# A hand-written order of work on one core: the delta rule's steps of the first head begin after class unit 9 instead of unit 13

## The chip, the core and the metric

One NeuronCore of a Trainium2 chip runs the whole program. The metric is the device time of one execution in microseconds (us); lower is better. All data is float32. Engines are named as in the profile: PE (TensorE, matrix multiplications), PEld (its weight loads), DVE (VectorE), ACT (ScalarE), POOL (GpSimd) and SP (SyncE, which here only issues transfers).

## The reference

One layer of a decoder with two mixers that work in parallel on the same normalised input, for a prompt of 2048 tokens and for 8 sequences of 4 new tokens. Cut to what the change touches, the prompt's mixers are:

```python
def hybrid_layer(x, ...):
    h = rmsnorm(x, norm_g)
    proj = jnp.einsum('bld,de->ble', h, w_in)
    # mixer a: gated delta rule, 4 heads of 128, evaluated in chunks
    qkv = causal_short_conv(x_ext, conv_w)
    o_a, s_new = gated_delta_rule(qa, ka, va, g, beta, s0)
    o_a = rmsnorm(o_a, dn_norm_g) * silu(z_a)
    # mixer b: causal windows at dilations 1, 4 and 16, 8 heads of 64, softmax merged over all three
    parts = [dilated_branch_prompt(qb, kb, vb, w // d, d) for w, d in DILATIONS]
    o_b = merge_dilations(parts) * silu(z_b)
    y = x + jnp.einsum('ble,ed->bld', concat(o_a, o_b), w_out)

def gated_delta_rule(q, k, v, g, beta, s0):      # per chunk
    sol = triangular_solve(eye + a_mat, rhs)     # needs the inverse of a unit lower triangle
    u, w = sol[..., :dv], sol[..., dv:]
    def step(S, xs):                             # strictly one chunk after the other
        v_new = u_c - w_c @ S
        o_c = q_c @ S + a_c @ v_new
        S = S * gl + k_c.T @ v_new
```

## The kernel before

The program has five stages, separated by barriers: `project` (the input projection), `gates`, `mixers`, `sample` and `output`. The change lies in `mixers`.

`mixers` handles the prompt in 16 chunks of 128 tokens (mixer a) and 8 attention heads (mixer b). It pairs them: while attention head h is finished, two delta chunks, 2h and 2h+1, are computed. Before the first head a preparation runs over all 16 chunks (`prepare`): decay matrices, key products, and the scores of head 0.

Each engine walks through the same list of steps in its own program (`walk`, L1189), and does in each step what is its part. An engine executes its instructions in the order in which they are written; a wait for a semaphore holds back everything that is written behind it. The list for the first head is `OPENING = head_order(True, True)` (L1063), for the others `BODY`. So `head_order` (L885) alone sets the order around the change. It makes two lists and weaves them:

- the attention steps. `turn k` transposes the k-th of 18 units of the exponentiated scores on PE (L1427), ACT evacuates it to `pt` and then issues one of 14 copies of the sample caches, DRAM to DRAM (`shift`, L1493 to L1496). `mix k` multiplies it with the values on PE (L1449), two units later. `score q` computes the q-th unit of the scores of the next head on PE (L1390 to L1397), and DVE scales and masks them (L1625, L1631); PE may be two score units ahead of DVE. `close r` adds two partial results on DVE (L1681), and POOL multiplies them with the gate (L1270). `near b` evacuates on ACT (L1529). `spread`, `swap` and `peak` form the row maxima of the next head.
- the 33 delta steps of `DELTA_ORDER` (L935), for chunk u of 0 and 1: three levels of `cross` (PE L1320, DVE L1579) and `double` (PE L1329 and L1330, DVE L1585 and L1587), which build the inverse of the 128-row triangle from inverses of its 16-row diagonal blocks; then the chain of the state, `ks`, `solve`, `av`, `su`, `qs` (PE L1339, L1353, L1364, L1358, L1347), and the norm of the output, `norm` (POOL L1252 to L1261) and `turn_o` (PE L1369, DVE L1613). `grow` is POOL's: it lays the 16-row inverses of the next chunk into a zeroed square (L1229).

The 16-row inverses of all chunks come from a substitution that only the opening has: the steps `sub` 1 to 15 and `flip` on DVE (L1567, L1569, L1674), which are ahead of `turn 8`. Their result is reordered through DRAM: SP writes it out (L1108, L1110), waits until both writes have landed, and reads it back in another shape (L1114). Meanwhile POOL, after the writes, zeroes `cross` (L1274), then waits for the reads and grows chunks 0 and 1 (L1229). Only then can PE start the first `cross` (its waits are at L1311 to L1314).

The delta steps are woven in by cost: each attention step has a cost in `head_order` (4 for a `turn`, 5 for a `score`, 8 for a `mix`, 10 each for the last three), and after each attention step as many delta steps are given as the share of the cost spent so far demands. In the opening the costs of all steps ahead of k = `FIRST_DELTA` are set to nothing, so that the delta steps begin there and are spread evenly over what is left:

```python
        if opening and k == FIRST_DELTA:
            cost = [0] * len(cost)
```

Of the kernel before, what the change touches and what calls it, by code (L numbers as in the profile page):

```python
# [843 lines left out]
LATEST = (1, 1, 3, 3, 5, 5, 7, 7) + (12,) * 5 + (17,) * 5  # L844
# [33 lines left out]


SUBS = 8  # L880
FIRST_NEAR = 9
FIRST_DELTA = 13


def head_order(more, opening=False):  # L885

    order, cost = [("exp", 0)], [0 if opening else 18]

    def add(c, *step):
        order.append(step)
        cost.append(c)

    for k in range(UNITS + LAG):
        if opening and k == FIRST_DELTA:
            cost = [0] * len(cost)
        if opening and 0 < k <= SUBS:
            for row in range(2 * k - 1, min(2 * k + 1, BASE)):
                add(0, "sub", row)  # L900
        if opening and k == SUBS:
            add(0, "flip")
        if k < UNITS:
            add(4, "turn", k)
            if k in FIRST and k != FIRST[-1]:
                add(0, "exp", FIRST.index(k) + 1)
            if more:
                for q in range(UNITS):
                    if k == (LATEST[q] if q >= 8 else FIRST_NEAR + q // 2 if opening else LATEST[q] + q % 2):
                        add(5, "score", q)  # L910
        if k >= LAG:
            m = k - LAG
            add(8, "mix", m)
            if m < 8 and m % 2:
                add(0, "near", m // 2)
            if m in (12, 17):
                for r in (0, 1) if m == 12 else (2, 3):
                    add(0, "close", r)
    if more:
        add(10, "spread")  # L920
        add(10, "swap")
        add(10, "peak")

    delta = [("delta",) + s for s in DELTA_ORDER if more or s[0] != "grow"]
    woven, spent, given = [], 0, 0
    for step, c in zip(order, cost):
        woven.append(step)
        spent += c
        upto = len(delta) * spent // sum(cost)
        woven += delta[given:upto]  # L930
        given = upto
    return woven
# [82 lines left out]
def mixers(nc, env, D):  # L1015

    with ExitStack() as ctx:
# [42 lines left out]
        shifted = sem("shifted")  # L1060
        S_CREDIT, T_CREDIT, C_CREDIT = 2, UNITS, 4
        BODY = [head_order(True), head_order(False)]
        OPENING = head_order(True, True)  # L1063
        PAIRS = SW_HEADS // 2
        block = ctx.enter_context(nc.Block())
# [1482 lines left out]
```

How the kernel before makes its waits and increments, by code:

```python
def at_least(eng, sem, n):  # L79
    if n > 0:
        eng.wait_ge(sem, n)
# [83 lines left out]
        @block.sync  # L166
# [11 lines left out]
            def load_x(n):  # L178
                if n >= XS:
                    sp.wait_ge(xT_done, 2 * (n - XS) + 2)
                if n < NT:
                    sp.dma_start(x_slot[n % XS], D.x[P * n:P * n + P, :]).then_inc(x_loaded[n % XS], 16)
                else:
                    sp.dma_start(x_slot[n % XS][0:NS, :], D.x_sample).then_inc(x_loaded[n % XS], 16)
# [1 line left out]
            def store_rows(n):  # L186
                sp.wait_ge(t_out, n + 1)
                sp.dma_start(D.new_v[P * n:P * n + P, :], stage[:, n % 2, :]).then_inc(stage_stored[n % 2], 16)
# [16 lines left out]
            with nc.allow_non_contiguous_dma(reason="a few weights, once"):  # L205
                for r in range(CONV_W):
                    sp.dma_start(conv_wt[:, :, r], D.conv_w[r].rearrange("(t p) -> p t", p=P)).then_inc(consts_in, 16)
            load_x(7)
            for n in range(8, NT + 1):
                load_x(n)
                store_rows(n - 8)
            load_w(1)
            for n in range(NT - 7, NT):
                store_rows(n)
            sp.wait_ge(v_sam_out, 1)
            for b in range(DEC_BATCH):
                sp.dma_start(D.out_v[b, PAST - DEC_SEQ:PAST, :], stage[DEC_SEQ * b:DEC_SEQ * b + DEC_SEQ, 0, :]).then_inc(rows_out, 16)
            def store_turned(j, kind, c):
                sp.wait_ge(tok_done, posts_before(j, kind, c) + 1)
                dst = {"k": D.k_tok, "v": D.v_tok, "wk": D.new_k}[kind]
```

## Time and profile before

| what | us |
|---|---|
| median of three runs | 2018.37 |
| lowest and highest run | 2014.06, 2027.25 |
| the profiled execution | 2027.25 |
| its span, first to last instruction in the profile | 2025.5 |

The profiled execution is the slowest of the three runs, 8.9 us above the median. It shows 27,818 instructions. PE is the engine with the most busy time. A busy PE in this profile is not a PE at its peak, since the clock that it is granted has two levels, shown in the views as 1.00 (2.4 GHz) and 0.50 (1.2 GHz), or as a mean between them for a stretch that has both. A timeline line gives the start, the length, the engine, the line of the kernel, what is written and read, how many like instructions were merged, and in brackets the idle time before it with what ended it. PE's instructions overlap, so the time from one start to the next says more than the length.

### The profile page before, as it was taken

To read this page: it belongs to the slowest core of one execution; us is meant where nothing else is said; L and a number is where in the kernel's file an instruction comes from. 1 tells how busy PE (TensorE), PEld (TensorE's weight loads), DVE (VectorE), ACT (ScalarE), POOL (GpSimd) and SP (SyncE) were. 2 spreads that over 40 slices of the span, in tenths; PEclk is the share of its full clock that TensorE was granted. 3 is DMA by queue.
4 is the path that set the end of the run, shared out by engine and by line. 5 is a ranking of instruction groups with operands and counts; after the bars stand their busy time and mean duration, and the time that the engine had idled before them with its cause. 6 is when DMAs were issued, how large, how long until landed. Compare 5 with 4: busy or idle time off the path is not lost. (4 is left out here: it accounts for less than half of the span.)

```text
span 2025.5 us, 27818 instructions
## 1 busy us (share of the span) xinstructions
PE 1745.5 (86%) x9674; PEld 1445.1 (71%) x9674; DVE 818.2 (40%) x1890; ACT 644.2 (32%) x1547; POOL 355.1 (18%) x367
## 2 busy tenths in 40 slices
PE   1999999999999999705788998998899468888897
PEld 1998888888888888604677887787788346666674
DVE  3424412511531351053743434544443445454462
ACT  3423311412321231111222443443444213333341
POOL 0000000000000000015123223313422343224231
PEclk9999999999999999958877988988998658999999
DMA  6321233344235333369774897797767456665660
GB/s 136 116 70 57 86 100 88 73 94 112 66 85 116 75 73 100 73 137 275 213 217 134 272 276 217 232 294 238 229 200 235 131 159 179 198 196 154 185 186 32
DMA packets 250191, 309.24 MB, mean 153 GB/s; under 512 B 70268, under 2 KB 198780, under 8 KB 240588
## 3 DMA queue, kind: packets, MB, share of 16 engines
q1 hardware_dynamic: 246484, 240.66, 44.5%
q10 hardware_dynamic: 3584, 66.98, 9.2%
q8 instruction: 72, 1.18, 0.2%
q14 instruction: 51, 0.42, 0.1%
HBM read 228.01 MB, written 146.44 MB: 185 GB/s over the span
## 5 line engine op out<-in xcount | busy, mean ns | idle before, releaser
L314 PE MATMUL pj<-hT_hi,w_hi 128*128 128x512 f32 x896 | 359.1, 401 | 1.8 <-DVE raw L541 1.8
L316 PE MATMUL pj<-hT_hi,w_lo 128*128 128x512 f32 x896 | 351.9, 393 | 0.0
L315 PE MATMUL pj<-hT_lo,w_hi 128*128 128x512 f32 x896 | 351.6, 392 | 0.0
L316 PEld LDWEIGHTS pj<-hT_hi,w_lo 128*128 128x128 f32 x896 | 168.3, 188 | 38.1
L314 PEld LDWEIGHTS pj<-hT_hi,w_hi 128*128 128x128 f32 x896 | 168.4, 188 | 36.8 <-issue 2.1
L315 PEld LDWEIGHTS pj<-hT_lo,w_hi 128*128 128x128 f32 x896 | 168.6, 188 | 34.5
L1449 PE MATMUL o_ps<-pt,vt 128*65 128x256 f32 (+3 forms) x560 | 154.4, 404 | 3.1 <-DVE ot L1681 2.1
L648 POOL IOTA row_at<- 128x1 int32 x1 | 0.1, 138 | 875.1 <-POOLq L2488 875.1
L1518 ACT ACTIVATE pt<-pt_ps 128x512 f32<-128x512 f32 x144 | 84.5, 587 | 184.3 <-PE pt_ps L1427 183.6
L2214 PE MATMUL y_bank<-wo_hi,mh 128*128 128x512 f32 (+1 forms) x272 | 113.4, 417 | 6.8 <-POOL ml L2199 4.6
L2215 PE MATMUL y_bank<-wo_lo,mh 128*128 128x512 f32 (+1 forms) x272 | 110.5, 406 | 0.0
L509 DVE SCALAR_TENSOR_TENSOR acc<-raw,conv_wt,acc 128x512 f32<-128x512 f32 x144 | 108.3, 752 | 5.1
L2216 PE MATMUL y_bank<-wo_hi,ml 128*128 128x512 f32 (+1 forms) x272 | 109.9, 404 | 0.0
L1449 PEld LDWEIGHTS o_ps<-pt,vt 128*65 128x65 f32 x560 | 75.4, 146 | 35.9 <-issue 25.0
L560 DVE TENSOR_TENSOR lo<-pj,hi 128x512 fp32r<-128x512 f32 x32 | 22.1, 692 | 156.5 <-ACT hi L472 156.5
L498 DVE TENSOR_TENSOR w_lo<-w_raw,w_hi 128x1024 fp32r<-128x1024 f32 x28 | 34.3, 1225 | 107.4 <-ACT w_hi L385 107.4
L1330 PE MATMUL d_ps<-tri,cross 128*128 128x64 f32 x384 | 76.9, 308 | 0.0
L1511 ACT ACTIVATE sc_near<-sc_near,ntop 128x256 f32<-128x256 f32 (+1 forms) x128 | 53.7, 490 | 68.3 <-DVE ntop L1660 65.6
L460 ACT ACTIVATE sil<-acc 128x512 f32<-128x512 f32 x48 | 30.4, 632 | 139.5 <-DVE acc L509 139.5
L1320 PE MATMUL d_ps<-tri,d_nt 128*128 128x64 f32 x384 | 61.7, 317 | 14.9 <-issue 8.9
L1631 DVE CUSTOM_DVE_ANT_0 sc_class<-s_ps,class_tab 128x512 f32<-128x512 f32 (+3 forms) x128 | 58.9, 488 | 32.4 <-PE s_ps L1397 21.9
L1320 PEld LDWEIGHTS d_ps<-tri,d_nt 128*128 128x128 f32 x384 | 59.8, 237 | 17.0 <-issue 16.9
(450 smaller groups left out, 3521.7 us busy)
## 6 DMA issues: line engine op xcount, KB each, us to landing
out_dram<-in_cache_k_win_dram ACTq DMA_DIRECT2D x56, 584.0 KB, 7.0
out_dram<-in_cache_v_win_dram ACTq DMA_DIRECT2D x56, 584.0 KB, 6.2
w_raw<-in_w_in_dram SPq DMA_DIRECT2D x32, 512.0 KB, 7.9
qk_ch<-sil SPq DMA_DIRECT2D x32, 256.0 KB, 2.4
z_ch<-xr SPq DMA_DIRECT2D x32, 256.0 KB, 2.5
wqk<-hi SPq DMA_DIRECT2D x32, 256.0 KB, 2.6
wqk<-lo SPq DMA_DIRECT2D x32, 256.0 KB, 2.9
sc_class<-qk_ch SPq DMA_DIRECT2D x32, 256.0 KB, 4.5
```

What stands on the lines that cost most here:

```text
L314: pe.matmul(out, w_hi[s][:, k, :], hT_hi[:, k, cols], start=(k == 0), stop=False)
L315: pe.matmul(out, w_hi[s][:, k, :], hT_lo[:, k, cols], start=False, stop=False)
L316: mm = pe.matmul(out, w_lo[s][:, k, :], hT_hi[:, k, cols], start=False, stop=(k == KT - 1))
L509: dve.scalar_tensor_tensor(out=a, in0=x(r), scalar=w(r), in1=a, op0=ALU.mult, op1=ALU.add).then_inc(chain if r < CONV_W - 1 else conv_done, 1)
L1320: mm = pe.matmul(d_ps[u][:, 64 * n:64 * n + 64], nt[u][:, n, :], blocks(tl[u], l, 0)[:, n], start=True, stop=True)
L1330: mm = pe.matmul(d_ps[u][:, 256 + 64 * n:256 + 64 * n + 64], x[:, n, :], blocks(tt[u], l, 1)[:, n], start=True, stop=True)
L1449: mm = pe.matmul(o_ps[g % 2][0:HD + 1, P * first:P * first + w], vt[:, n, :], pt[:, k % CUTS, at:at + w], start=opened, stop=False, skip_g ...
L1518: act.activation(pt[:, k % CUTS, 0:w], pt_ps[k % 2][:, 0:w], ACT.Copy).then_inc(S["turned_out"], 1)
L1631: ins = dve.tensor_tensor_reduce(sc_class[:, r, class_at(b):class_at(b + 1)], s_ps[k % 2][:, at:at + w], E.class_tab[:, CHUNK - w:], SCALE ...
L2214: pe.matmul(y_ps[0:rows, :], mh[:, u, k, 0:rows], w_hi[:, k, cs], start=(k == 0), stop=False)
L2215: pe.matmul(y_ps[0:rows, :], mh[:, u, k, 0:rows], w_lo[:, k, cs], start=False, stop=False)
L2216: mm = pe.matmul(y_ps[0:rows, :], ml[:, u, k, 0:rows], w_hi[:, k, cs], start=False, stop=(k == KT - 1))
```

## The change

`FIRST_DELTA` goes from 13 to 9, and the constant `FIRST_NEAR`, which was 9 and sets where the first score units of head 1 stand, is replaced by `FIRST_DELTA`, so that the score units keep their places. All that moves are the 33 delta steps of the opening. The list of `BODY` is the same. The file has one line less, so that all lines behind it have a number smaller by one in the changed kernel.

```diff
 SUBS = 8
-FIRST_NEAR = 9
-FIRST_DELTA = 13
+FIRST_DELTA = 9
...
-                    if k == (LATEST[q] if q >= 8 else FIRST_NEAR + q // 2 if opening else LATEST[q] + q % 2):
+                    if k == (LATEST[q] if q >= 8 else FIRST_DELTA + q // 2 if opening else LATEST[q] + q % 2):
```

The opening from `flip` on, as the function gives it before (exp, near and rest left out, of which the last does nothing on any engine; `x:u` is a delta step x of chunk u):

```text
flip turn8 mix6 turn9 score0 score1 mix7 turn10 score2 score3 mix8 turn11 score4 score5 mix9 turn12 score6..score12 mix10
turn13 cross0:0 mix11 cross0:1 double0:0 turn14 double0:1 mix12 cross1:0 cross1:1 turn15 double1:0 mix13 double1:1 cross2:0
turn16 cross2:1 mix14 double2:0 double2:1 turn17 ks:0 score13 qs:0 score14 solve:0 score15 score16 av:0 su:0 score17 mix15
ks:1 norm:0 mix16 solve:1 mix17 turn_o:0 qs:1 close close spread su:1 av:1 swap grow:1 norm:1 peak turn_o:1
```

and now:

```text
flip turn8 mix6 turn9 score0 cross0:0 score1 mix7 cross0:1 turn10 double0:0 score2 double0:1 score3 mix8 cross1:0 turn11
cross1:1 score4 double1:0 score5 mix9 double1:1 turn12 cross2:0 score6 cross2:1 score7 score8 double2:0 score9 double2:1
score10 score11 ks:0 score12 qs:0 mix10 solve:0 turn13 mix11 turn14 av:0 mix12 su:0 close close turn15 grow:0 mix13 ks:1
turn16 mix14 norm:0 turn17 solve:1 score13 score14 score15 turn_o:0 score16 qs:1 score17 mix15 su:1 mix16 av:1 mix17
grow:1 close close spread norm:1 swap turn_o:1
```

On PE, from `turn 9` on (first row; `pt_ps` is where it is turned to). The rows with `s_ps` are scores, those with `o_ps<-pt,vt` are `mix 7`. Before:

```order
L1427 MATMUL pt_ps<-ident,sc_class 128x128 x4
L1390 MATMUL s_ps<-kh,qs 128x128
L1391 MATMUL s_ps<-kl,qs 128x128
L1390 MATMUL s_ps<-kh,qs 128x256
L1391 MATMUL s_ps<-kl,qs 128x256
L1390 MATMUL s_ps<-kh,qs 128x256
L1391 MATMUL s_ps<-kl,qs 128x256
L1390 MATMUL s_ps<-kh,qs 128x256
L1391 MATMUL s_ps<-kl,qs 128x256
L1449 MATMUL o_ps<-pt,vt 65x256
L1449 MATMUL o_ps<-pt,vt 65x128 x2
L1427 MATMUL pt_ps<-ident,sc_class 128x128 x4
```

and in the changed kernel:

```order
L1426 MATMUL pt_ps<-ident,sc_class 128x128 x4
L1389 MATMUL s_ps<-kh,qs 128x128
L1390 MATMUL s_ps<-kl,qs 128x128
L1389 MATMUL s_ps<-kh,qs 128x256
L1390 MATMUL s_ps<-kl,qs 128x256
L1319 MATMUL d_ps<-tri,d_nt 128x64 x4
L1389 MATMUL s_ps<-kh,qs 128x256
L1390 MATMUL s_ps<-kl,qs 128x256
L1389 MATMUL s_ps<-kh,qs 128x256
L1390 MATMUL s_ps<-kl,qs 128x256
L1448 MATMUL o_ps<-pt,vt 65x256
L1448 MATMUL o_ps<-pt,vt 65x128 x2
```

The first `cross` (`d_ps<-tri,d_nt`) now stands behind four rows of scores; before it stood 60 rows further down, behind `turn 13`.

On PE, from `mix 15` to the end of the first head (`L1369` and then `L1368` are `turn_o`, `wide,fold` is `swap`). Before:

```order
L1449 MATMUL o_ps<-pt,vt 65x512
L1339 MATMUL d_ps<-d_state,kq 128x128 x4
L1449 MATMUL o_ps<-pt,vt 65x384
L1449 MATMUL o_ps<-pt,vt 65x128
L1353 MATMUL d_ps<-four,tri 128x128 x4
L1449 MATMUL o_ps<-pt,vt 65x256 x2
L1369 MATMUL d_ps<-ident,d_oo 128x128 x4
L1347 MATMUL d_ps<-d_state,kq 128x128 x4
L1358 MATMUL d_ps<-four,ktok 128x128 x4
L1364 MATMUL d_ps<-four,d_attn 128x128 x4
L1405 MATMUL s_ps<-wide,fold 128x64 x2
L1369 MATMUL d_ps<-ident,d_oo 128x128 x4
```

and in the changed kernel, to `turn_o` of chunk 1:

```order
L1448 MATMUL o_ps<-pt,vt 65x512
L1357 MATMUL d_ps<-four,ktok 128x128 x4
L1448 MATMUL o_ps<-pt,vt 65x384
L1448 MATMUL o_ps<-pt,vt 65x128
L1363 MATMUL d_ps<-four,d_attn 128x128 x4
L1448 MATMUL o_ps<-pt,vt 65x256 x2
L1404 MATMUL s_ps<-wide,fold 128x64 x2
L1368 MATMUL d_ps<-ident,d_oo 128x128 x4
```

The last `mix` is now followed by `swap` and `turn_o` alone; before, four more delta steps stood between.

On POOL, the end of the first head, from the product that `su` of chunk 1 needs (`four<-four,dl`). `zb` are the two gates of `close`, the rows with `ors` and `d_oo` are `norm` of chunk 1. Before:

```order
L1242 TENSOR_TENSOR four<-four,dl 128x512
L1270 TENSOR_TENSOR zb<-ot,zb 64x512 x2
L1229 TENSOR_TENSOR tri<-inv_t,own 128x512
L1229 TENSOR_TENSOR tri<-inv_l,own 128x512
L1252 TENSOR_TENSOR ors<-oss,rq 128x4
L1255 TENSOR_SCALAR ors<-ors 128x4
L1257 TENSOR_TENSOR ors<-ors,halves 128x4
L1259 TENSOR_TENSOR ors<-ors,rq 128x4
L1261 TENSOR_TENSOR d_oo<-d_oo,ors 128x512
```

and in the changed kernel:

```order
L1241 TENSOR_TENSOR four<-four,dl 128x512
L1228 TENSOR_TENSOR tri<-inv_t,own 128x512
L1228 TENSOR_TENSOR tri<-inv_l,own 128x512
L1269 TENSOR_TENSOR zb<-ot,zb 64x512 x2
L1251 TENSOR_TENSOR ors<-oss,rq 128x4
L1254 TENSOR_SCALAR ors<-ors 128x4
L1256 TENSOR_TENSOR ors<-ors,halves 128x4
L1258 TENSOR_TENSOR ors<-ors,rq 128x4
L1260 TENSOR_TENSOR d_oo<-d_oo,ors 128x512
```

`grow` now stands ahead of the gates; `norm` stands behind them in both.

## Rows read from the trace of the kernel before

**Rows 1.** Part 1 of the page, busy time of each engine.
```profile
PE 1745.5 (86%) x9674; PEld 1445.1 (71%) x9674; DVE 818.2 (40%) x1890; ACT 644.2 (32%) x1547; POOL 355.1 (18%) x367
```

**Rows 2.** Timeline of PE around the first inverses; start, length, engine, line, operation, idle before.
```profile
1017.11 0.31 PE L1390 MATMUL s_ps<-kh,qs 128*128 128x128 f32 x1
...
1017.65 0.28 PE L1390 MATMUL s_ps<-kh,qs 128*128 128x256 f32 x1
...
1020.50 0.30 PE L1390 MATMUL s_ps<-kh,qs 128*128 128x128 f32 x1 [0.90 <-DVE top L1625]
...
1033.42 0.60 PE L1427 MATMUL pt_ps<-ident,sc_class 128*128 128x128 f32 x4
1039.91 1.94 PE L1320 MATMUL d_ps<-tri,d_nt 128*128 128x64 f32 x8 [5.89 <-issue]
```

**Rows 3.** Timelines of DVE, SP and POOL, the same stretch.
```profile
1018.76 1.04 DVE L1674 COPY cross<-cross 128x1024 f32<-128x1024 f32 x1
...
1019.83 0.33 SPq L1110 DMA_DIRECT2D inv_all<-cross  x1
...
1029.37 2.70 POOL L1274 MEMSET cross<- 128x1536 f32 x2 [53.14 <-DMA inv_all<-cross]
1037.75 1.05 POOL L1229 TENSOR_TENSOR tri<-inv_t,own 128x512 f32<-128x512 f32 x1 [5.67 <-DMA inv_l<-inv_all]
```

**Rows 4.** Timeline of ACT, two of three cache copies that it issues there.
```profile
1019.64 0.54 ACTq L1496 DMA_DIRECT2D out_dram<-in_cache_v_win_dram  x1
...
1025.72 0.52 ACTq L1496 DMA_DIRECT2D out_dram<-in_cache_v_win_dram  x1
```

**Rows 5.** DMA view of 1018 to 1030 us; packets, MB, share of 16 engines.
```profile
q10 hardware_dynamic: 194, 3.44, 73.8%
q1 hardware_dynamic: 288, 1.05, 21.6%
```

**Rows 6.** Stretches; us, busy and count by engine, granted clock, DMA share, GB/s.
```profile
1018.00:1040.00 22.00, 14.08 (x80) 11.26 (x78) 11.12 (x50) 7.62 (x15) 4.95 (x5) 0.91 1.00 322
1040.00:1073.70 33.70, 33.70 (x144) 30.24 (x145) 6.75 (x16) 1.79 (x3) 7.81 (x7) 0.50 0.38 85
1073.70:1100.00 26.30, 19.07 (x130) 16.82 (x129) 14.86 (x43) 7.03 (x29) 15.96 (x19) 0.95 0.44 104
...
1102.00:1114.70 12.70, 12.23 (x55) 11.68 (x56) 3.23 (x13) 5.00 (x11) 0.64 (x1) 0.50 0.94 308
1173.90:1185.60 11.70, 10.06 (x46) 9.70 (x47) 2.59 (x11) 6.47 (x15) 2.04 (x2) 0.50 0.96 331
```

**Rows 7.** Timeline of PE, the same kinds of step at each clock.
```profile
1061.69 1.92 PE L1449 MATMUL o_ps<-pt,vt 128*65 128x512 f32 x2
1063.40 0.52 PE L1329 MATMUL d_ps<-cross,tri 128*128 128x64 f32 x2
...
1120.95 1.02 PE L1449 MATMUL o_ps<-pt,vt 128*65 128x256 f32 x4
1121.81 0.33 PE L1329 MATMUL d_ps<-cross,tri 128*128 128x64 f32 x2
```

**Rows 8.** Timeline of PE, the end of the first head.
```profile
1088.52 1.03 PE L1449 MATMUL o_ps<-pt,vt 128*65 128x256 f32 x4
...
1094.28 0.56 PE L1405 MATMUL s_ps<-wide,fold 128*128 128x64 f32 x4
1100.31 1.11 PE L1369 MATMUL d_ps<-ident,d_oo 128*128 128x128 f32 x4 [5.47 <-POOL d_oo L1261]
```

**Rows 9.** Timelines of DVE and POOL, the same end.
```profile
1090.69 1.27 DVE L1681 TENSOR_TENSOR ot<-o_ps,ot 65x512 f32<-65x512 f32 x2
...
1091.45 3.65 POOL L1270 TENSOR_TENSOR zb<-ot,zb 64x512 f32<-64x512 f32 x2 [0.77 <-DVE ot L1681]
...
1097.11 0.19 POOL L1252 TENSOR_TENSOR ors<-oss,rq 128x4 f32<-128x4 f32 x1
...
1099.21 1.04 POOL L1261 TENSOR_TENSOR d_oo<-d_oo,ors 128x512 f32<-128x512 f32 x1
```

## The prediction

> **What bounds the kernel now.** I read the busy times first, then the granted clock in stretches, then the timeline of PE around the place of the change, and only then the other engines there. PE has 86% of the span in busy time, the next engine 40% [rows 1]. In the opening head the timeline of PE is nearly gapless but for two holes: 5.89 us ahead of the first `cross` at 1039.91, and 5.47 us ahead of the last `turn_o` at 1100.31 [rows 2, 8]. Since every head follows on PE's one list, a delay of that last `turn_o` should delay all behind it. So I take its start as the mark: 1100.31 before, and the change is worth what it moves that mark.
>
> The first hole is the way of the 16-row inverses. DVE's `flip` ends at 1018.76 + 1.04 = 1019.80; SP issues the second write at 1019.83; the writes have landed when POOL is released at 1029.37; the reads when it starts `grow` at 1037.75 [rows 3]. PE's `cross` follows after two of POOL's four `grow` operations of 1.05 us each, at 1039.91 [rows 2]. That way takes 20.1 us from the end of `flip`, and nothing on PE's list shortens it. In the kernel before, PE fills 14 us of it, to 1034.0, with score units, turns and mixes [rows 2].
>
> The reader is to see a second thing in the stretches: after that hole PE has a clock of 0.50 (1.2 GHz) from 1040 to 1073.7, for 33.7 us, although it is busy for all of them [rows 6]. What it does there is `cross` and `double`, with a mix or a turn between. In the next heads, where scores, turns and mixes are interleaved with the same steps, the low level holds for 12.7 us (1102 to 1114.7) and 11.7 us (1173.9 to 1185.6) [rows 6].
>
> **The change, part by part.**
>
> *The work that loses its cover.* PE now reaches `cross` at 1017.65, behind the first score unit, and stands until the inverses have come [rows 2]. What it did from there to 1034 must be done later: score units 1 to 12, mixes 7 to 10, turns 10 to 13. Between 1018 and 1040 PE is busy for 14.08 us [rows 6]; nothing between 1034 and 1039.91 is in that. So +14.1 us, at the full clock. DVE, ACT and POOL have nothing that could go ahead: their scores, evacuations and gates all wait for PE.
>
> *The way of the inverses gets shorter.* In it ACT issues three cache copies (turns 10 to 12), from 1019.64 to 1025.72 [rows 4]. They now come behind PE's wait. From 1018 to 1030 the queue of these copies (q10) held the 16 DMA engines for 73.8% of 12 us with 3.44 MB, and SP's queue (q1), which has the inverses, for 21.6% [rows 5]. One copy of 584 KB is then 0.584/3.44 x 8.86 = 1.5 us of all engines, three are 4.5 us. The bounds are 0 (the transfers wait for memory, not for engines) and -4.5 us. I take -3, since the writes landed 9.5 us after their issue in this crowd. The first `cross` then starts at about 1036.9, and PE stands for 19 us where it stood for 5.9.
>
> By the Trainium skill (DMA: Bandwidth & Descriptors, section "Issuing engines are not separate DMA queues") transfers that different engines start interleave on the same 16 DMA engines. The shares of the two queues above agree, and by the rule alone the term would be the whole -4.5.
>
> *The clock.* After the longer hole PE will again be at 1.2 GHz. Then it meets `cross`, a score unit, a mix, `cross`, a turn, `double`, a score unit and so on, which resembles the later heads, where the low level held for 12 us [rows 6]. I take 15 us, some more than there, since the new list has fewer turns between the delta steps than those heads. At the low level a mix takes 63.40 - 61.69 = 1.71 us from start to start, at the high one 121.81 - 120.95 = 0.86 us (times above 1000) [rows 7], so a microsecond at the low level does half a microsecond's work. Before: 33.7 us low. Saved: (33.7 - 15)/2 = -9.4 us. Bounds: at 12 us low, -10.9; at 34 us low, 0.
>
> *Small waits in the middle.* From 1073.7 to 1100 PE is idle for 26.30 - 19.07 = 7.2 us, of which 5.5 are the second hole, so 1.8 us are small waits [rows 6, 8]. In the new order `close`, `grow` and `norm` of chunk 0 come right after each other on POOL, at 3.65 + 2.1 + 3.1 us [rows 9, 3], behind `mix 12`, and PE has about 8 us of work from there to `turn_o` of chunk 0. Laying the lists of PE, DVE and POOL beside each other with these durations, I get 2.4 us of waiting there, and some 0.8 us at score units 8 to 11, where PE waits for DVE's masks as it does at 1020.50 for 0.90 us [rows 2]. That makes 3.2 against 1.8: +1.4 us, with 0 and +4 as bounds.
>
> *The second hole.* `norm` of chunk 1 waits in both orders behind POOL's two gates, which wait for the last mix. The last mix starts at 1088.52 and ends about 0.9 us later, and `turn_o` comes at 1100.31, 10.9 us behind its end, of which 5.47 are idle [rows 8]. Now `turn_o:0`, `qs`, `su` and `av` stand ahead of that mix and no longer fill the time. From its end: about 0.3 us of signalling and DVE's first addition (half of 1.27 us), POOL's two gates (3.65 us), then `norm` 3.1 us (1097.11 to 1100.25) [rows 9], and about 0.2 to signal PE, in all 7.9 us, with half a microsecond of `swap` in it. The hole is about 7.5 us where it was 5.5: +2.0 us. `grow`, which stood between gates and `norm`, is ahead of them now; that gain of 2.1 us is in the 7.9.
>
> The sum is 14.1 - 3 - 9.4 + 1.4 + 2.0 = +5.1 us for the profiled execution, from 2027.25 to 2032.4. Its time is 8.9 us above the median of the runs shown, and nothing of that lies in the terms, so I put the same difference to the median: 2018.4 + 5.1 = 2023.5 us. Nothing in the later heads changes its order, and their transfers keep their distance from the mark.
>
> **The rivals.**
>
> *The clock stays low (slower than forecast).* The mark of 33.7 us came from a stretch with one mix and one turn in about ten microseconds (four mixes from 1041 to 1072, of which [rows 7] has one). If sparse scores aren't enough to change that, PE stays at 1.2 GHz through all of `cross` and `double`, 34 us or more. The clock term is then 0, and the sum +14.5 us: 2033. For it speaks that this stretch was fully busy and still low; against it that two heads with nearly the same mixture rose after 12 us.
>
> *The clock comes back at once, and the delta steps are covered (faster).* In this case the low level lasts for some 3 us. The saving is (33.7 - 3)/2 = 15.4 us, the round trip gives all of its 4.5, and the small waits stay as they are: 14.1 - 4.5 - 15.4 + 0 + 2.0 = -3.8 us, 2014.6. It decides from a low stretch of under 11 us on: there 14.1 - 4.5 - 11.6 + 2.0 is zero. Against it is that no head's beginning rose sooner than after 11.7 us.
>
> The Trainium skill (TensorE: Matmul & The Clock Gate, section "What's actually happening") has it that the gate opens after sustained work of PE. By that rule this rival would hold, with 2014.6; but the 33.7 busy microseconds at 0.50 [rows 6] don't agree with it, and the measurement decides.
>
> *The order is absorbed.* A later wait could eat the delay, for instance the operands of the next chunks. Then nothing is seen: 2018.4. Against it: in the next head PE is busy 12.23 of 12.70 us right after the mark [rows 6], so there is no slack to take it.
>
> *The change doesn't do what it says.* If `cross` did not wait for the inverses, the wait at 1017.65 would not arise and only the interleaving would be left, about -9 us. The code excludes it: the wait for POOL's `grow` is ahead of it.
>
> **How the numbers follow.** Main case 0.55, clock low 0.2, clock back at once 0.13, absorbed 0.1, something unnamed 0.02. A measurement of this kernel can tell about 1% from no change, 20 us; its own three runs lie within 13. The terms' own bounds give 14.1 - 4.5 - 10.9 + 0 + 1 = -0.3 at one end and, with 22 us low, 14.1 + 0 - 6 + 4 + 3 = +15 at the other; with the rivals and some microseconds of scatter of a median the range is 2011 to 2036 us. Slower by over 1% (above 2038.6) needs the low clock and bad luck: 0.07. Faster by over 1% (below 1998) has no term that would carry it: 0.02. Within 1%: 0.91.
>
> **What would show each step.** Right: PE's first `cross` comes directly behind one score unit, with an idle time of 18 to 22 us ahead of it and its start near 1037; no cache copy is issued in this hole; the low clock from about 1021 on lasts some 15 us beyond the first `cross`; `turn_o` of chunk 0 waits about 2 us for POOL, that of chunk 1 about 7.5; the mark lies near 1105 to 1107. The next heads look as before, shifted. Wrong: an inverse that lands before 1034 or after 1040 (the transfer term), a low level of under 8 or over 25 us after `cross` (the clock term), a mark that has moved by 5 us without the total following (the absorbed case).

## The result and the profile after

The changed kernel takes 2026.17 us (median of 12 runs, 2023.1 to 2029.8), the kernel before in runs beside it 2014.42 us (12 runs, 2006.9 to 2027.3). The ratio is 1.0053 with a 95% interval of 1.0035 to 1.0072: slower by about 11 us, within 1%. The forecast was 2023.5 us with a range of 2011 to 2036 and a difference of +5.1.

The two profiled executions, however, are equally long: a span of 2025.5 us before and of 2025.1 after. So a comparison of these two traces can't show where 11 us come from. What it does show is that PE's waits came where the prediction put them, and that the clock did not do what it said. PE in the opening head after the change, as a timeline (start, length, engine, line, operation, idle before it with its releaser):

```profile
1016.67 0.28 PE L1390 MATMUL s_ps<-kl,qs 128*128 128x256 f32 x1
1035.77 1.94 PE L1319 MATMUL d_ps<-tri,d_nt 128*128 128x64 f32 x8 [18.82 <-issue]
...
1083.94 1.12 PE L1368 MATMUL d_ps<-ident,d_oo 128*128 128x128 f32 x4 [1.97 <-POOL d_oo L1260]
...
1095.71 0.66 PE L1404 MATMUL s_ps<-wide,fold 128*128 128x64 f32 x4 [1.75 <-DVE wide L1641]
1101.70 1.12 PE L1368 MATMUL d_ps<-ident,d_oo 128*128 128x128 f32 x4 [5.33 <-POOL d_oo L1260]
```

These answer to [rows 2, 8]. The first `cross` stands behind one score unit and waits for 18.82 us where it waited for 5.89. `turn_o` of chunk 0 now waits for POOL's `norm`, 1.97 us. `turn_o` of chunk 1 waits for 5.33 us behind `swap`, which itself waited for 1.75.

The way of the inverses, from the timelines of DVE, SP and POOL, against [rows 3]:

```profile
1017.61 1.04 DVE L1673 COPY cross<-cross 128x1024 f32<-128x1024 f32 x1
...
1018.67 0.33 SPq L1109 DMA_DIRECT2D inv_all<-cross  x1
1026.18 0.37 SPq L1113 DMA_DIRECT2D inv_t<-inv_all  x1
...
1033.61 1.05 POOL L1228 TENSOR_TENSOR tri<-inv_t,own 128x512 f32<-128x512 f32 x1 [4.70 <-DMA inv_l<-inv_all]
```

The writes land 7.5 us after their issue, where it was 9.5, and from `flip` to the first `cross` it is 1035.77 - 1017.61 = 18.16 us, where it was 21.15.

The clock in stretches, against [rows 6] (us; busy time and count of PE, PEld, DVE, ACT, POOL; granted clock, DMA share, GB/s):

```profile
1035.77:1042.40 6.63, 6.63 (x29) 6.25 (x30) 1.59 (x6) 0.59 (x1) 4.91 (x5) 0.50 1.02 219
1042.40:1083.00 40.60, 37.88 (x275) 34.20 (x273) 21.68 (x77) 10.88 (x28) 8.88 (x11) 1.00 0.38 104
1083.00:1090.30 7.30, 6.36 (x23) 5.25 (x24) 2.31 (x9) 1.14 (x4) 3.91 (x4) 0.53 0.45 131
```

Behind the hole PE is at 1.2 GHz (0.50) for 6.6 us only, and then again for 6.9 us, nearly all of the third stretch, behind the new wait of `turn_o`; before it was 33.7 us in one piece. A low stretch of under 8 us after `cross` was one of the prediction's own signs that its clock term was wrong. The mark, the start of the last `turn_o`, lies at 1101.70 and not at 1105 to 1107.

In what follows, three starts are the marks in each trace: F, DVE's copy that ends the inverses (`flip`); C, PE's first `cross`; M, the `turn_o` of chunk 1 in the opening head. "Low behind C" is how long the granted clock stays at 0.50 behind C, read in stretches of 0.5 us.

### The profile page after: what moved, and what is told of

Its sections match the earlier page's. It is cut to its first block and busy times, and to the rows that moved or that the text cites. A ratio compares the mean times of both kernels' runs of the same rounds, so it can differ in the third digit from the quotient of the medians.

```text
span 2025.1 us, 27818 instructions
## 1 busy us (share of the span) xinstructions
PE 1734.0 (86%) x9674; PEld 1435.7 (71%) x9674; DVE 818.3 (40%) x1890; ACT 644.4 (32%) x1547; POOL 355.2 (18%) x367
## 5 line engine op out<-in xcount | busy, mean ns | idle before, releaser
L1510 ACT ACTIVATE sc_near<-sc_near,ntop 128x256 f32<-128x256 f32 (+1 forms) x128 | 53.7, 490 | 71.3 <-DVE ntop L1659 68.7
L1329 PE MATMUL d_ps<-tri,cross 128*128 128x64 f32 x384 | 71.6, 291 | 0.0
```

Source lines behind the costliest of these rows:

```text
L1329: mm = pe.matmul(d_ps[u][:, 256 + 64 * n:256 + 64 * n + 64], x[:, n, :], blocks(tt[u], l, 1)[:, n], start=True, stop=True)
```

## The experiments

Each kernel ran on a chip beside the kernel before; `b_` kernels start from the kernel before, `a_` kernels from the changed one.

**b_again and b_again2: the kernel before, unchanged.** No edit.

> The kernel before, unchanged, profiled once more. Theory (clock): the 12 times of before reach from 2006.9 to 2027.3 us, those of the changed kernel only from 2023.1 to 2029.8, because in before PE's low clock after the 5.9 us hole lasts for a different time from execution to execution. The profiled execution of 2027.25 us had 33.7 us of it. One that takes 2010 to 2016 us should show a low stretch shorter by twice the difference, 5 to 14 us, and the rest alike. Rival (elsewhere): the scatter of before comes from transfers or from other stages; then a faster execution shows about 34 us at the low clock again and is shorter in another place.

> The kernel before once more, for a third look at the clock. Clock theory: from the copy that ends the inverses (flip) to the last turn_o of the opening head the time is 65.5 us (what b_warm shows without any low clock there) plus half of the low stretch behind the hole (10 us gave 70.1, 37.5 us gave 81.6), so that this profile too lies on that line within 1.5 us. Rival: some other value with the same low stretch.

b_again: median 2017.45 us of 12 runs, 2005.4 to 2032.7, ratio 1.0021 (0.9987 to 1.0055), which is the kernel against itself. Its profiled execution took 2011.2 us. The view of stretches and the timeline of PE:

```profile
1041.85:1047.00 5.15, 5.15 (x21) 4.33 (x21) 0.42 (x1) 0.00 (x0) 3.92 (x4) 0.50 1.02 215
1047.00:1084.50 37.50, 34.06 (x253) 30.64 (x252) 20.24 (x57) 6.82 (x26) 16.60 (x17) 1.00 0.40 91
...
1088.60 1.12 PE L1369 MATMUL d_ps<-ident,d_oo 128*128 128x128 f32 x4 [5.48 <-POOL d_oo L1261]
```

The low clock behind C lasts 5.2 us here where the first profile of the same kernel had 33.8. From C to M it is 46.75 us instead of 60.40, and the time is 16 us lower. The second repeat, b_again2 (one execution, 2024.3 us), has

```profile
1040.89:1057.00 16.11, 16.11 (x70) 14.61 (x71) 2.35 (x6) 0.60 (x1) 3.92 (x4) 0.51 0.78 164
...
1092.71 1.11 PE L1369 MATMUL d_ps<-ident,d_oo 128*128 128x128 f32 x4 [5.47 <-POOL d_oo L1261]
```

16.1 us of low clock, and 51.82 us from C to M. F to M is 72.5 us. The line of the expectation counts the low clock within the hole too, some 17 us in all, and gives 74.0, so this profile is just within its 1.5. The first profile is not: 65.5 plus half of its 37.5 us would be 84.3, and it has 81.6. The three traces are of the same program, with the same wait ahead of M (5.47 and 5.48 us). So the kernel before has a lottery in its opening head, and the profile that the prediction was made from had drawn the worst of three. It isn't the only lottery: b_again2 has 17.7 us less of the low clock behind C than the first profile and 9.0 us less from F to M, but it is only 3.0 us faster. Its F comes 1.4 us later, and what follows M takes 4.6 us more (929.8 us for 925.2).

**b_warm and a_warm: the hole filled.** PE gets matmuls whose result nobody reads, just ahead of the first `cross`; nothing is left out.

```diff
+        OPENING.insert(OPENING.index(("delta", "cross0", 0)), ("warm", 24))      # a_warm: 80
...
+                elif step == "warm":
+                    for _ in range(a[0]):
+                        pe.matmul(d_ps[0][:], E.ident_r[:], heads(E.shut), start=True, stop=True)
```

> Before, with 24 matmuls of 128x512 whose results nobody reads put on PE ahead of the first cross of the opening head, into the 5.9 us hole (about 5.2 us of work). Clock theory: PE keeps 2.4 GHz behind the hole, the time is about that of the fastest executions of before, 2005 to 2009 us, and its scatter is under 8 us. Rival (elsewhere): median within 3 us of before's 2014 and the scatter still 15 to 20 us.

> The changed kernel, with 80 such matmuls in the 18.8 us hole ahead of its first cross (about 17.3 us of work). The clock is taken out on both sides, so that a_warm against b_warm is the price of the order alone. By the prediction's terms without the clock that is 14.1 (work that lost its cover) - 3.7 (inverses earlier, as seen) + 1.4 + 2.0 = about +14 us, so a_warm at 2019 to 2024 us. Against the changed kernel it saves half of the 6.6 us low stretch behind the hole, 3 us. Rival (the delta chain gains from sitting between attention steps): a_warm is only 3 to 8 us above b_warm, since at the full clock the packed order of before waits more for DVE.

In the traces both kept the clock at 2.4 GHz from the start of `cross` on. In b_warm it falls only in the wait ahead of M, where PE has nothing to do. In a_warm it falls once more, for 3.4 us of work behind the wait of the first `turn_o` (the last line shown of a_warm):

```profile
1036.91 1.08 PE L1321 MATMUL d_ps<-tri,d_nt 128*128 128x64 f32 x8 [0.18 <-issue]
...
1081.40 1.12 PE L1370 MATMUL d_ps<-ident,d_oo 128*128 128x128 f32 x4 [5.48 <-POOL d_oo L1262]
...
1036.91:1077.50 40.59, 36.86 (x272) 32.87 (x272) 20.85 (x59) 7.02 (x27) 20.72 (x21) 1.00 0.51 125
...
1293.00:1320.00 27.00, 25.52 (x112) 23.89 (x113) 6.79 (x25) 9.41 (x21) 2.65 (x3) 0.50 0.97 281
```

```profile
1035.89 1.08 PE L1320 MATMUL d_ps<-tri,d_nt 128*128 128x64 f32 x8 [0.88 <-issue]
...
1080.90 0.66 PE L1369 MATMUL d_ps<-ident,d_oo 128*128 128x128 f32 x4 [1.97 <-POOL d_oo L1261]
...
1097.81 1.12 PE L1369 MATMUL d_ps<-ident,d_oo 128*128 128x128 f32 x4 [5.33 <-POOL d_oo L1261]
...
1035.89:1083.00 47.11, 43.46 (x315) 39.52 (x316) 24.40 (x84) 11.48 (x29) 16.83 (x19) 1.00 0.49 120
1083.00:1086.50 3.50, 3.50 (x13) 2.42 (x12) 1.17 (x8) 1.14 (x4) 0.87 (x1) 0.53 0.84 237
```

F starts at 1015.98 in b_warm and at 1017.80 in a_warm. F to M is then 65.4 us against 80.0: the new order costs 14.6 us, where the prediction's terms without the clock gave 14.5. From C to M it is 44.49 against 61.92, that is +17.4, and from F to C 20.93 against 18.09, that is -2.8. Part of this is clock even so: 3.4 us of work at half the speed are 1.7 us. Without them the order costs 12.9 us, of which +15.7 lie from C to M. The rival that expected 3 to 8 us, because the packed order of before should wait more for DVE, falls.

The times did less. b_warm has a median of 2014.49 us (ratio 0.9996, 0.9964 to 1.0028) and still runs from 2006.9 to 2026.1: my expectation of 2005 to 2009 was wrong, and the rival, a median within 3 us of before and the same scatter, describes the times. The last line of b_warm's stretches gives a reason for the execution that was profiled: a later head, the fourth behind the opening, stayed at 1.2 GHz for 27 us, where heads usually have 10 to 14. What the other eleven executions had, no trace shows. a_warm has 2021.56 us (ratio 1.0022, 0.9996 to 1.0049), inside its range, and lies 7 us over b_warm; with this scatter the medians can't confirm the 14.6 us of the traces. That was left to the runs with the clock held everywhere.

**a_norm: POOL's order at the end.** The changed kernel with

```diff
+        OPENING.remove(("delta", "norm", 1))
+        OPENING.insert(OPENING.index(("close", 2)), ("delta", "norm", 1))
```

> The changed kernel with one delta step moved: in the opening, norm of chunk 1 stands ahead of the last two close steps, as in the list of the later heads, so that POOL does not do two gates (3.65 us) ahead of it. If POOL's order makes the second hole (5.3 us ahead of the last turn_o), the time falls by about 3 us, 2023 us, and the hole is 2 to 2.5 us, PE then waiting for ACT's squares and the norm alone. Rival: the hole is set by the squares of ACT anyway, and nothing moves.

```profile
1098.32 1.11 PE L1370 MATMUL d_ps<-ident,d_oo 128*128 128x128 f32 x4 [2.35 <-POOL d_oo L1262]
```

The wait ahead of M falls from 5.33 to 2.35 us, so POOL's two gates ahead of `norm` make 3 us of that hole. F to M falls from 84.1 to 81.5 us, which alone would prove little, since a_again below, without the edit, has 81.7; but the low clock is as long here as in the first profile of the changed kernel (6.9 us behind `cross`, and another 6.9 later). The time, 2025.12 us (ratio 1.0045, 1.0015 to 1.0076), for 2023 expected, has moved by 1 us against the changed kernel, which the interval doesn't tell from none or from three.

**b_copies: the cache copies out of the way.** In the kernel before, for head 0 alone:

```diff
+                    if isinstance(h, int) and h == 0 and 10 <= k <= 12:
+                        k = 2 * PIECES
+                    elif isinstance(h, int) and h == 0 and k >= 15:
+                        k -= 5
```

> Before, with the three cache copies of turns 10 to 12 issued with turns 15 to 17 instead, so that they are out of the way of the inverses. If they cost the way of the inverses what the changed kernel's trace shows (19.3 against 16 to 17 us from the copy of DVE to POOL's grow), the first cross comes 3 us earlier and the hole shrinks from 6 to 8 us to 3 to 5. The low clock behind it stays a matter of luck, or is shorter on average with a shorter hole. Median 3 to 6 us below before. Rival (the way waits for memory, not for engines): the time from flip to grow stays at 19 us, and nothing moves.

```profile
1018.67 0.33 SPq L1110 DMA_DIRECT2D inv_all<-cross  x1
1027.51 0.37 SPq L1114 DMA_DIRECT2D inv_t<-inv_all  x1
...
1037.08 1.94 PE L1320 MATMUL d_ps<-tri,d_nt 128*128 128x64 f32 x8 [3.73 <-issue]
```

The writes land 8.8 us after their issue, where the three traces of before have 9.5, 12.0 and 10.7 us. With F at 1017.58, F to C is 19.50 us, against 21.15, 23.39 and 20.72 before and 18.16 in the changed kernel. So by this one trace the copies are about 2 us of the 3 to 4 that the inverses gained, against a scatter of 2.7 us before; the rest is open. The hole was 3.73 us and the clock was low behind it all the same, for 15.9 us. Median 2013.57 us beside 2018.55, ratio 0.9973 (0.9939 to 1.0007): 5 us less, as expected (3 to 6), but the interval doesn't tell it from nothing.

**fd11 and fd15: other places.** `FIRST_DELTA` at 11 and at 15, `FIRST_NEAR` left at 9.

> Before with FIRST_DELTA = 11, the score units kept: the first cross stands behind score 4, about 5 us of PE's work later than in the changed kernel. Theory (work that loses its cover): of the 14 us about 9 to 10 remain uncovered and two of the three copies are back in the way of the inverses, so flip to the last turn_o takes 79 to 82 us and the median lies 6 to 9 us over before, between both kernels. Rival (any hole that drops the clock costs the same): as slow as the changed kernel, 11 us over before. Rival (interleaving pays once the hole is shorter): within 3 us of before.

> Before with FIRST_DELTA = 15, the score units kept: turn 14, 15 and mix 11, 12 stand ahead of the first cross and fill about 3 us of its hole, so that 2 to 4 us of it are left. Theory: less uncovered waiting and a hole too short to drop the clock for certain: median 3 to 8 us below before, with less scatter, flip to the last turn_o at 63 to 70 us. Rival (the delta chain gets too dense): the 33 steps have fewer attention steps between them, PE waits for DVE and POOL at the end by as much as the hole lost, and the time is that of before.

```profile
1038.66 1.73 PE L1320 MATMUL d_ps<-tri,d_nt 128*128 128x64 f32 x7 [15.56 <-issue]
...
1038.66:1046.50 7.84, 7.84 (x34) 7.02 (x35) 1.63 (x6) 0.00 (x0) 4.91 (x5) 0.51 1.03 217
...
1096.67 1.11 PE L1369 MATMUL d_ps<-ident,d_oo 128*128 128x128 f32 x4 [4.89 <-POOL d_oo L1261]
```

fd11's hole is 15.56 us, its F to M (from 1017.97) 78.7 us, and its median 2022.50 us, 3.7 us below the changed kernel's and 4 us over its neighbours of before (2018.55), with a ratio of 1.002 (0.999 to 1.005). Both are a little under what was expected, 79 to 82 us and 6 to 9 us over before. Trace and order of the values fit the lost cover; the interval alone would also allow no difference.

```profile
1040.88 1.08 PE L1320 MATMUL d_ps<-tri,d_nt 128*128 128x64 f32 x8 [2.99 <-issue]
...
1040.88:1055.50 14.62, 14.62 (x66) 12.79 (x66) 2.35 (x6) 0.60 (x1) 7.86 (x7) 0.54 0.88 183
...
1090.00:1120.50 30.50, 26.14 (x116) 24.33 (x117) 6.67 (x24) 9.21 (x22) 5.76 (x8) 0.50 0.77 226
```

fd15's hole is only 2.99 us, but the clock fell all the same, 1.2 us behind C and for 13.5 us, once more for 3.5 us ahead of M, and again for 30.5 us at the next head. F to M (from 1019.40 to 1093.31) is 73.9 us, not the 63 to 70 expected, and no better than b_again2. Median 2021.12 us, ratio 0.9988 (0.9954 to 1.0021). The expected 3 to 8 us didn't come: a shorter hole bought nothing here.

**b_warmall and a_warmall: the clock held in every head.** As b_warm and a_warm, and in addition

```diff
+        OPENING.insert(OPENING.index(("swap",)) + 1, ("warm", 24, 0))
+        OPENING.append(("warm", 4, 0))
+        for body in BODY:
+            body.insert(body.index(("delta", "cross0", 0)) + 1, ("warm", 10, 0))
+        BODY[0].insert(BODY[0].index(("swap",)), ("warm", 7, 0))
+        BODY[0].append(("warm", 4, 0))
...
+                    spare = d_ps[0] if a[1] else pt_ps[0]
```

> b_warm with idle matmuls in the holes of PE at the end of every head too (24 behind swap in the opening, 7 ahead of swap, 4 behind the last turn_o and 10 behind the first cross of every later head), each a little shorter than the hole it fills. Clock theory: PE holds 2.4 GHz through the mixers, every later head loses its 10 to 14 us at 1.2 GHz and so takes 64 to 67 us instead of 71.7, the median is 35 to 50 us below before, 1970 to 1982, and the scatter of the mixers is gone. Rival: the matmuls lengthen the holes they fill by more than the clock gives back, 2010 us or more.

> The same additions in the changed kernel (80 ahead of its first cross). With the clock held on both sides, the medians of a_warmall and b_warmall should differ by the price of the order, 14.6 us in the traces of a_warm and b_warm: +12 to +17 us. Rival (the difference of the two medians came from the low clock behind the 18.8 us hole): under 5 us.

b_warmall: 1990.36 us (7 runs), ratio 0.986 (0.9832 to 0.9889). a_warmall: 2005.01 us (8 runs), ratio 0.9945 (0.9918 to 0.9972). The difference of the medians is 14.65 us, and that of F to M in the traces of b_warm and a_warm was 14.6. The price of the order is thereby measured in two ways. It has in it what the new wait of `turn_o` does to the clock: a_warmall's trace has 6.9 us at 1.2 GHz there, a_warm's 3.4. The rival (under 5 us) falls. The gain of 25 us over before is less than the 35 to 50 I expected. From the last `turn_o` of one head to that of the next, the kernel before takes 71.5 to 71.7 us in the second to the sixth head. In b_warmall's trace three of the six heads between the opening and the last take 67.2 to 67.9 us, the others 71.2, 71.6 and 76.2. The longest has PE waiting for ACT's exponentials behind its second `turn`, a wait that I had not filled, and low clock from a microsecond later; other heads have the same wait (1.20 us in the second) and keep the clock:

```profile
1171.23 0.63 PE L1438 MATMUL pt_ps<-ident,sc_near 128*128 128x128 f32 x4 [1.20 <-ACT sc_near L1522]
...
1239.35 0.63 PE L1438 MATMUL pt_ps<-ident,sc_near 128*128 128x128 f32 x4 [1.45 <-ACT sc_near L1522]
...
1240.50:1258.00 17.50, 17.50 (x77) 15.98 (x77) 4.69 (x18) 4.74 (x11) 1.77 (x2) 0.51 0.91 259
```

The profiled execution was the slowest of the seven (2011.5 us): there the inverses were late (25.8 us from F to C), the 24 matmuls left 5.0 us of the hole open, and the clock fell for 17 us:

```profile
1032.76 5.73 PE L1424 MATMUL d_ps<-shut,ident_r 128*128 128x512 f32 x24
1043.49 1.94 PE L1327 MATMUL d_ps<-tri,d_nt 128*128 128x64 f32 x8 [5.00 <-issue]
```

**b_best: both together.** b_warmall with 30 matmuls ahead of the first `cross`, and the edit of b_copies.

> b_warmall with 30 instead of 24 idle matmuls ahead of the first cross, and the three cache copies out of the way of the inverses as in b_copies. In the profiled execution of b_warmall the inverses came 25.8 us after flip and the 24 matmuls left 5 us of the hole open, behind which the clock fell for 17 us. With the copies away the way is 1 to 2 us shorter, and 1.3 us more of it are filled: median 1 to 4 us below b_warmall's 1990, with no execution over 2005. Rival: the copies only move their load under the operands of the next head, and the median is 1990 or more.

1989.88 us (6 runs, 1985.3 to 1990.9), ratio 0.9873 (0.9851 to 0.9894), about 25 us faster than before and 36 faster than the changed kernel. From C to M the clock is whole, and F to M 66.05 us. Five of the six heads between the opening and the last take 67.1 to 68.1 us, one 71.3:

```profile
1042.36:1086.00 43.64, 41.57 (x296) 37.03 (x295) 21.83 (x59) 8.84 (x32) 21.21 (x24) 1.00 0.60 165
...
1153.00:1221.00 68.00, 65.53 (x453) 56.83 (x453) 32.12 (x109) 31.53 (x78) 22.24 (x25) 1.00 0.86 264
```

Against b_warmall no gain of the median is seen (0.5 us for the expected 1 to 4); no execution over 2005 was among the six, but six are few. In this trace the 30 matmuls did harm: the inverses were ready at 1039.7, where POOL ends its second `grow`, and `cross` started only behind the matmuls, at 1042.36:

```profile
1035.44 7.08 PE L1424 MATMUL d_ps<-shut,ident_r 128*128 128x512 f32 x30
1038.64 1.06 POOL L1236 TENSOR_TENSOR tri<-inv_l,own 128x512 f32<-128x512 f32 x1
```

**a_again: the changed kernel once more.** No edit.

> The changed kernel once more, for a second look at its clock. If its small scatter comes from a low stretch that ends at once behind the hole in every execution, this profile has 5 to 8 us at 1.2 GHz behind its first cross and flip to the last turn_o in 82.5 to 85.5 us, as in the first (84.1). Rival: it varies like that of before, by 5 us or more.

```profile
1035.27:1039.50 4.23, 4.23 (x18) 3.84 (x19) 1.20 (x5) 0.00 (x0) 4.23 (x5) 0.52 1.02 215
...
1099.13 1.11 PE L1368 MATMUL d_ps<-ident,d_oo 128*128 128x128 f32 x4 [5.34 <-POOL d_oo L1260]
```

The low clock behind C is 4.2 us (5 to 8 were expected), F to M from 1017.41 is 81.7 us, a little under the range of 82.5 to 85.5. So the low stretch is as short as in the first trace, and the two differ by 2.4 us from F to M, not by the 5 or more of the rival. Two traces are few to call that a rule.

The opening heads in one table (us):

| kernel | F to C | C to M | low behind C | F to M |
|---|---|---|---|---|
| before, first profile | 21.15 | 60.40 | 33.8 | 81.55 |
| b_again2 | 20.72 | 51.82 | 16.1 | 72.54 |
| b_again | 23.39 | 46.75 | 5.2 | 70.14 |
| b_warm | 20.93 | 44.49 | 0 | 65.42 |
| changed, first profile | 18.16 | 65.93 | 6.6, later 6.9 | 84.09 |
| a_again | 17.86 | 63.86 | 4.2, later 3.4 | 81.72 |
| a_warm | 18.09 | 61.92 | 0, later 3.4 | 80.01 |

Within the order of before, C to M is 44.5 us plus nearly half of the low stretch: half would give 47.1 for 5.2 us (measured 46.75), 52.5 for 16.1 (51.82), 61.4 for 33.8 (60.40). With half of all low stretches taken off, the changed order has 59.2, 60.1 and 60.2 us from C to M.

## Why the prediction was right or wrong

The sign and the likeliest outcome (within 1%) were right, and the time lies in the range. The size of the difference was half of what was measured. The mechanism was right in its waits; the clock term held for the execution that was traced, but not for the median.

- *The work that loses its cover, +14.1; small waits, +1.4; the second hole, +2.0.* Together 17.5 us from C to M at the full clock. a_warm against b_warm shows +17.4, but 1.7 of that is clock. Without it, it is +15.7, and the profiled pair gives the same: 60.40 - 16.9 = 43.5 and 65.93 - 6.75 = 59.2. So the three terms are 1.8 us too large. The second hole, 5.33 + 1.75 us for 5.47, is +1.6. The waits in the middle are 1.13, 0.56 and 1.97 us in a_warm (2.4 had been estimated for the last, at `turn_o` of chunk 0) against 2.1 us in all in b_warm, so +1.6. What remains, 12.5 for 14.1, falls to the cover by subtraction; no run measured it alone. Two readings of the prediction are off by 0.3 us each, in opposite directions: PE's work from 1017.65 and not from 1018 on is 14.4 us, and the stretch with the small waits ends 0.3 us before the hole does, so that they were 2.1 us and not 1.8.
- *The inverses come earlier, -3.* In the profiled pair 21.15 - 18.16 = 3.0 us, between b_warm and a_warm 2.8. The named cause is about two thirds of it at most: b_copies took only the copies away and got to 19.5, and before by itself scatters from 20.7 to 23.4.
- *The clock, -9.4.* I had put 15 us of low clock behind `cross`. It was 6.6, and then 6.9 behind the wait of `turn_o`, which I had priced as a wait of 2.4 us but not as a place where the clock falls: 13.5 in all, right in the sum by luck and not in its parts. Against the 33.8 us of before that gives back 10.2 us, and 15.7 - 10.2 is the 5.5 us by which C to M rose in the profiled pair. The rival in which the clock comes back at once was nearer behind `cross` (3 us), but its result, faster by 4 us, needed the 33.7 us of before to be the rule.
- *The sum for the profiled execution, +5.1.* Measured in the two traces from F to M: 15.7 - 3.0 - 10.2 = +2.5 us.
- *The step that failed: "Its time is 8.9 us above the median of the runs shown, and nothing of that lies in the terms, so I put the same difference to the median."* The largest term rested on 33.7 us at 1.2 GHz, and two more profiles of the same kernel had 5.2 and 16.1 us behind C. With the mean of the three, 18.4 us, the clock term would have been (18.4 - 13.5)/2 = -2.5 us, and the sum 15.7 - 3.0 - 2.5 = +10.2 us. Measured are +11.7 by the medians of 12 and 12 runs, and 10.7 by the ratio (7 to 14.5). How much of the miss this explains is argued and not shown. Three draws between 5 and 34 us fix no mean, and b_warm speaks against the full amount: 18.4 us of low clock less should make its median 9 us lower than before's, and it was 0.8 us lower by the ratio (7 lower to 6 higher).
- *Absorbed later:* from M to the last `turn_o` it is 484.5 us before and 482.5 after. That gain lies in the next head, from one last `turn_o` to the next: 70.1 us before, 67.5 after, with 5 us less of low clock. In the four traces with the changed order or nearly so (a_norm, a_warm and a_again too) this head takes 67.3 to 67.5 us, in the three of before 68.0 to 70.6. So some 2 us of the delay do come back there, against the prediction's "The next heads look as before, shifted". With an F that is 1.15 us earlier, this is why the two profiled executions are equally long.

What stays open is why the order of before is slow to return to the high clock, from 5 to 34 us, where the changed order returned after 4 to 7 us in three traces, a_norm's among them. The changed order has scores between its `cross` and `double` steps and that of before has none. That fits, and fd11, which has some there, had 7.7 us; but all of these also have the long hole, and no run separated the two. Why the three profiles of before differ at all is open, and so is the last microsecond of the inverses' way.

## What to carry to other kernels

Read the profiled execution against the scatter of the runs before a term is taken from it. When it lies 9 us above the median, look for what could have been unlucky in it, such as a long stretch at the low clock, and bound the forecast by a lucky execution as well. When independent work is moved behind a wait for something that only time brings (here a trip through DRAM), the cost is the work that used to lie beside it, and it can be counted off the timeline of before. Where PE has holes of 2 to 8 us between dense stretches, matmuls that nobody reads can be worth more than a better order: 25 us of 2015 here, where the order was worth 14.6. Their number is a choice between two losses: 24 left 5.0 us of a late hole open, and 30 held up an early `cross` by 2.6 us.

## What the runs showed of the hardware

- The same program with the same waits had 5.2, 16.1 and 33.8 us at 1.2 GHz behind a hole of 5.5 to 8 us, and the times of the kernel ran from 2005 to 2036 us over all its runs. The length of the hole didn't decide it: the longest of the three, 8.12 us, had the shortest low stretch, and fd15's hole of 2.99 us was followed by 13.5 us.
- PE was 100% busy in the low stretches ([rows 6], and 16.11 of 16.11 us in b_again2). So in these traces PE's busy time doesn't tell when the high clock returns. The Trainium skill (TensorE: Matmul & The Clock Gate, section "HAM oscillation — how this bites in real kernels") has the cost of holes that repeat as clock lost behind each; by that the trace agrees: filling those at the ends of the heads took five of the six heads between the opening and the last in b_best to 67.1 to 68.1 us, where before had 70.1 to 71.7.
- A copy from DRAM to DRAM on ACT's queue lengthens a short round trip on SP's: the writes of 1 MB landed after 8.4 and 8.8 us where only the last three copies were moved (b_best, b_copies), after 7.3 to 8.0 in the changed order, which has them elsewhere too, and after 9.5 to 12.9 with them.
